# The gate evacuation's walk order: key by key instead of token by token

## The chip, the cores and the metric

The kernel runs on one core of a Trainium2 chip. The metric is the device time of one execution in microseconds (us), the median of several runs. Engines are called as in the profile: PE is the matrix engine (TensorE), PEld its weight loads, DVE is VectorE, ACT is ScalarE, POOL is GpSimd, SP is SyncE; ACTq and SPq are the queues on which ACT and SP issue their DMA transfers. A line of the kernel is written L1143.

## The reference, cut to what matters

The program is one step of a decoder layer for 512 prompt tokens and 32 sample tokens (D_MODEL = 1024): a modulated RMSNorm, one input projection, a convolution group and an mLSTM group, an output projection, and then a retrieval layer (PEER) over 128 x 128 single-neuron experts. The change sits in the retrieval layer:

```
q = (xb @ w_pq).reshape(PEER_BLOCK, PEER_HEADS, 2, PEER_DHALF)
s = jnp.einsum('thpd,phnd->thpn', q, sub_keys)
s1, i1 = lax.top_k(s[:, :, 0], PEER_TOPK)
s2, i2 = lax.top_k(s[:, :, 1], PEER_TOPK)
...
top, pos = lax.top_k(cand, PEER_TOPK)
eidx = jnp.take_along_axis(cidx, pos, axis=-1)
gate = jax.nn.softmax(top, axis=-1)
a = jnp.einsum('thkd,td->thk', u_tab[eidx], xb)
act = (jax.nn.gelu(a) * gate)
out = jnp.einsum('thk,thkd->td', act, v_tab[eidx])
```

Each token takes 8 x 16 experts out of 16384, and each has a gate weight.

## The kernel before, in words

For 416 of the 544 tokens the kernel does not gather: it computes the product of the tokens with all 16384 experts and multiplies the result by a gate matrix that is zero where an expert was not retrieved. The remaining 128 tokens are done by gathered rows on DVE (the functions `dot` and `row_add`, on the tile `ug`), threaded between other work.

The expert table comes in 256 blocks of 512 KB (`tab`). ACT makes the rounded high part of each (`t_hi`, L1092, tile `tHi`), POOL the low part (`lo_part`, L612, tile `tLo`), and PE does 24 matmuls of 416 columns per block (`product`, L866). Blocks 0 to 127 (the first half) are the u table: ACT applies gelu to the result (L1133, tile `ga`) and stores it to a scratch tensor in HBM (L1136, `gelu_scratch`). Blocks 128 to 255 are the v table: gelu and gates come back from HBM, are multiplied, and are PE's operands.

The gate matrix is built during blocks 57 to 116 of the first half. There are 52 steps of 8 tokens (`STEP_TOK`), and `gate_steps(n)` spreads them over the blocks, one behind most products and none behind some. In each step DVE makes one-hot tiles (`one_hots`, L1552 to L1556); PE does one matmul of 128 x 128 for each of the 8 tokens (`gate_product`, L876, shown in the trace as 16 instructions) and writes banks 4 and 5 of PSUM, laid out as 8 tokens by 128 keys, keys innermost; ACT then reads both banks and writes the result into the SBUF tile `stage` (L1143). `stage` has the shape [128 partitions, 2, 128 keys, 32 tokens] in float32: tokens are innermost, and the step's 8 tokens are neighbours of each other there. Four steps fill one half of `stage`, and behind the fourth ACT issues a DMA transfer of 2 MB to `gate_scratch` (L1148). There are 13 of these.

The order of ACT's work in a block n is written out by hand: gelu of block n, the high part of block n+3, the issue of the gelu store (L1136), then the gate step's evacuation (L1143), and behind every fourth one the issue of the gate store (L1148). Both stores are issued on ACT's own queue, so an issue that takes long holds up the evacuation behind it. PE's order is: product of block n, then the gate product of the step. The gate product of step st waits until the evacuation of step st-1 is done (`s_gev`, L873), since there is one pair of banks for it.

Of the kernel before, what the change touches and what calls it, by code (L numbers as in the profile page):

```python
# [9 lines left out]
ACT = mybir.ActivationFunctionType  # L10
AXX = mybir.AxisListType.X

P = 128
# [48 lines left out]
STEP_TOK = TB // 4  # L62
# [31 lines left out]
def gate_steps(n):  # L94

    return [st for st in range(NSTEP) if G_FIRST + st * G_SPAN // NSTEP == n]
# [24 lines left out]
def build(nc, a, o):  # L121
    with ExitStack() as ctx:
# [145 lines left out]
        def peer(name, shape, dt=F32):  # L268
            n = 4
            for q in shape[1:]:  # L270
                n *= q
            t = at(name, shape, zp[0], dt)
            zp[0] += -(-n // 32) * 32
            assert zp[0] <= C_AT + 26400, name
            return t
# [14 lines left out]
        stage = peer("stage", [P, 2, NKEY, TB])  # L290
# [16 lines left out]
        ps = ctx.enter_context(nc.psum_tensor("ps", [P, 8, 512], F32))  # L307
# [21 lines left out]
        def sem(name):  # L329
            return ctx.enter_context(nc.semaphore(name))  # L330
# [91 lines left out]
        s_gev = sem("gate_evacuated")  # L422
# [484 lines left out]
        def _(act):  # L907
            link = linker(act, s_ach)
            f = nc.scalar.activation
# [179 lines left out]
            def t_hi(n):  # L1089

                act.wait_ge(s_tab[n % TABS], 16 * (n // TABS + 1))
                nc.scalar.copy(tHi[:, n % SPL], tab[:, n % TABS]).then_inc(s_thi, 1)  # L1092

            def gelu_copy(c):

                act.wait_ge(s_gin[c % 4], 16 * (c // 4 + 1))
                if c >= 2:
                    act.wait_ge(s_alo, c - 1)
                elif c == 0:
                    act.wait_ge(s_gev, NSTEP)  # L1100
                nc.scalar.copy(ps[:, 4 + c % 2, 0:TD], gin[:, c % 4]).then_inc(s_gcp, 1)

            def act_hi(c):

                act.wait_ge(s_a32, c + 1)
                nc.scalar.copy(actHi[c // GRP % 2][:, c % GRP], ps[:, 4 + c % 2, 0:TD]).then_inc(s_ahi, 1)
# [23 lines left out]
            for n in range(NCH):  # L1130
                act.wait_ge(s_prod, n + 1)
                act.wait_ge(s_gas[n % 2], 16 * (n // 2 + 1))
                f(ga[:, n % 2], ps[:, n % 2, 0:TD], ACT.Gelu_apprx_tanh).then_inc(s_gelu, 1)  # L1133
                t_hi(n + 3)
                act.wait_ge(s_gelu, n + 3)
                act.dma_start(ga_dram[n], ga[:, n % 2]).then_inc(s_gas[n % 2], 16)  # L1136
                if n == N_SHUF - 2:
                    act.wait_ge(s_top, NST)
                    f(best[:, 0], best[:, 0], ACT.Exp).then_inc(s_gexp, 1)
                for st in gate_steps(n):  # L1140
                    b, j = st // 4, st % 4
                    act.wait_ge(s_gmm, st + 1)
                    f(stage[:, b % 2, :, STEP_TOK * j:STEP_TOK * (j + 1)].rearrange("p c t -> p t c"),  # L1143
                      ps[:, 4:6, :].rearrange("p b (t c) -> p (b t) c", c=P), ACT.Identity).then_inc(s_gev, 1)
                    if j == 3:
                        act.wait_ge(s_gev, st + 1)
                        act.wait_ge(s_gst2, 16 * (b + 1))
                        act.dma_start(gt_dram[:, :, b, :].rearrange("q p (c t) -> p q c t", c=4),  # L1148
                                      stage[:, b % 2].rearrange("p (q c) t -> p q c t", c=4)).then_inc(s_gst2, 16)
                if n >= NCH - GRP:  # L1150
                    c = n - NCH + GRP
                    if c == 0:
                        gelu_copy(0)
                    gelu_copy(c + 1)
                    act_hi(c)

            for n in range(NCH, NT):
# [3 lines left out]
                c = n - NCH + GRP  # L1161
# [525 lines left out]
```

## Time and profile before

| | |
|---|---|
| median of 3 runs | 1866.88 us (1865.66 to 1868.56) |
| profiled execution, its own time | 1866.18 us |
| its span in the trace | 1864.5 us |
| PE busy | 1780.4 us, 95% of the span |
| POOL busy | 1083.0 us, 58% |
| DVE busy | 1183.9 us, 63% |
| ACT busy | 728.1 us, 39% |
| mean granted TensorE clock | 0.978 of full speed |

The span is the time from the first to the last instruction that the profiler saw; the profiled execution's own time is 1.7 us longer. The busy time of an engine says how much of the span it worked, not whether the end of the program waits for it. For that the profile has the chain of work that ended last, followed back from the last instruction to what released each step, and a list of waits: which engine waited at which line, and for what.

### The profile page before, as it was taken

The numbers are of one execution on the slowest core, as the hardware profiler recorded it, in microseconds if no ns is written. First come the engines' busy times: TensorE is split into PE (matmuls) and PEld (weight loads), VectorE is DVE, ScalarE is ACT, GpSimd is POOL, SyncE is SP. The second block draws the span as 40 slices with busy tenths as digits, with TensorE's granted clock in tenths as the row PEclk, the third lists the DMA queues.
The fourth block names the chain that finished last, engine by engine and source line by source line (L and its number), as shares of the span: only waits on it lengthen the run. The fifth ranks groups of instructions, "written<-read, shape, count | busy, mean of one in ns | idle before, by whom it ended". The sixth has DMA issues, their size and how long they took to land.

```text
span 1864.5 us, 27254 instructions
## 1 busy us (share of the span) xinstructions
PE 1780.4 (95%) x10594; PEld 1698.5 (91%) x10594; DVE 1183.9 (63%) x2350; ACT 728.1 (39%) x983; POOL 1083.0 (58%) x612
## 2 busy tenths in 40 slices
PE   7899999799999999999999998999999999999995
PEld 3899887688999999999999998989999999999995
DVE  3441343627898799985666665446677777777746
ACT  2454232323333333354554544443444444444431
POOL 1667221132337788854554454477877888887851
PEclk9899999899999999999999999999999999999997
DMA  8545121233215888868687786799999999999951
GB/s 273 172 148 170 62 97 57 75 113 103 91 51 163 273 275 281 275 211 276 233 269 242 250 260 217 228 400 369 363 353 357 377 350 377 353 368 361 364 185 48
DMA packets 191200, 442.39 MB, mean 237 GB/s; under 512 B 20064, under 2 KB 106080, under 8 KB 190816
## 3 DMA queue, kind: packets, MB, share of 16 engines
q1 hardware_dynamic: 82320, 251.88, 39.5%
q0 software_dynamic: 36864, 134.23, 19.4%
q10 hardware_dynamic: 71888, 54.53, 8.8%
q8 instruction: 84, 1.38, 0.3%
q14 instruction: 44, 0.36, 0.1%
HBM read 381.42 MB, written 59.17 MB: 236 GB/s over the span
## 4 chain that ended last, share of the span: by engine, by line
PE 87%; DVE 4%; DMA 3%; ACTq 2%; ACT 2%; issue 1%; POOL 1%; SPq 0%; DVEq 0%; POOLq 0%
PE ps L866 57%; PE ps L652 17%; PE ps L876 5%; ACTq L1136 2%; PE ps L672 2%; PE ps L681 1%; DMA gelu_scratch<-ga 1%; PE ps L841 1%; ACT stage L1143 1%; DMA tab<-in_tab 1%; DMA raw<-in_w 1%; ACT tHi L1092 1%; PE ps L764 0%; DMA ug<-in_urows,eidx 0%; PE ps L798 0%
## 5 line engine op out<-in xcount | busy, mean ns | idle before, releaser
L612 POOL TENSOR_TENSOR tLo<-tab,tHi 128x1024 fp32r<-128x1024 f32 x256 | 635.5, 2482 | 357.9 <-ACT tHi L1092 356.5
L1092 ACT CAST tHi<-tab 128x1024 fp32r<-128x1024 f32 x256 | 267.9, 1047 | 331.9 <-PE ps L866 321.1
L866 PE MATMUL ps<-actHi,tLo 128*128 128x416 f32 x1024 | 361.7, 353 | 5.5 <-issue 5.3
L866 PE MATMUL ps<-hHi,tLo 128*128 128x416 f32 x1024 | 364.5, 356 | 0.0
L866 PE MATMUL ps<-hLo,tHi 128*128 128x416 f32 x1024 | 361.6, 353 | 0.0
L866 PE MATMUL ps<-actHi,tHi 128*128 128x416 f32 x1024 | 359.6, 351 | 0.0
L866 PE MATMUL ps<-hHi,tHi 128*128 128x416 f32 x1024 | 358.8, 350 | 0.0
L866 PE MATMUL ps<-actLo,tHi 128*128 128x416 f32 x1024 | 357.4, 349 | 0.0
L600 POOL TENSOR_TENSOR wLo<-raw,wHi 128x1024 fp32r<-128x1024 f32 x53 | 127.7, 2409 | 316.0 <-ACT wHi L930 316.0
L866 PEld LDWEIGHTS ps<-actHi,tLo 128*128 128x128 f32 x1024 | 192.5, 188 | 7.6 <-issue 5.6
L866 PEld LDWEIGHTS ps<-hHi,tHi 128*128 128x128 f32 x1024 | 193.2, 189 | 2.8
L866 PEld LDWEIGHTS ps<-actLo,tHi 128*128 128x128 f32 x1024 | 192.9, 188 | 2.9
L866 PEld LDWEIGHTS ps<-hHi,tLo 128*128 128x128 f32 x1024 | 193.1, 189 | 1.5
L866 PEld LDWEIGHTS ps<-hLo,tHi 128*128 128x128 f32 x1024 | 192.4, 188 | 1.6
L866 PEld LDWEIGHTS ps<-actHi,tHi 128*128 128x128 f32 x1024 | 193.1, 189 | 0.8
L652 PE MATMUL ps<-hHi,wLo 128*128 128x272 f32 x848 | 180.9, 295 | 11.5 <-DVE hLo L1200 7.9
L1427 DVE SCALAR_TENSOR_TENSOR ug<-ug,ps 128x1024 f32<-128x1024 f32 x128 | 154.9, 1217 | 57.2 <-DMA ug<-in_urows,eidx 56.3
L1133 ACT ACTIVATE ga<-ps 128x416 f32<-128x416 f32 x128 | 66.7, 521 | 310.1 <-PE ps L866 282.0
L1589 DVE SCALAR_TENSOR_TENSOR xT<-ps,mod,xT 128x416 f32<-128x416 f32 x128 | 83.3, 651 | 152.3 <-PE ps L866 152.3
L652 PE MATMUL ps<-hHi,wHi 128*128 128x272 f32 x848 | 176.9, 290 | 0.0
L652 PE MATMUL ps<-hLo,wHi 128*128 128x272 f32 x848 | 176.6, 290 | 0.0
L1437 DVE SCALAR_TENSOR_TENSOR ps<-ug,act_s,ps 128x1024 f32<-128x1024 f32 x127 | 162.8, 1282 | 3.7 <-DVE ps L1437 0.5
(310 smaller groups left out, 2617.8 us busy)
## 6 DMA issues: line engine op xcount, KB each, us to landing
tab<-in_tab SPq DMA_DIRECT2D x256, 512.0 KB, 6.1
raw<-in_w SPq DMA_DIRECT2D x101, 512.0 KB, 3.9
gelu_scratch<-ga ACTq DMA_DIRECT2D x128, 208.0 KB, 4.4
gate_scratch<-stage ACTq DMA_DIRECT2D x13, 2048.0 KB, 14.1
gt<-gate_scratch SPq DMA_DIRECT2D x32, 832.0 KB, 5.8
gin<-gelu_scratch SPq DMA_DIRECT2D x128, 208.0 KB, 7.8
xT<-in_xT SPq DMA_DIRECT2D x1, 2176.0 KB, 10.0
out_y<-yo SPq DMA_DIRECT2D x8, 272.0 KB
```

The lines of the kernel that those rows point to most:

```text
L600: pool.tensor_tensor(wLo[:, i % 2], raw[:, p % RAW], wHi[:, i % 2].bitcast(F32), ALU.subtract).then_inc(s_wlo, 1)
L612: pool.tensor_tensor(tLo[:, n % SPL], tab[:, n % TABS], tHi[:, n % SPL].bitcast(F32), ALU.subtract).then_inc(s_tlo, 1)
L652: last = mm(pair(n)[:, h], w, x[:, k, h * HF:(h + 1) * HF], start=first, stop=end)
L672: last = mm(ps[0:NSEQ, mod_bank(m), 0:2 * P], cT[:, k, :], raw[:, p:p + 2, k, :], start=(k == 0), stop=(k == KT - 1))
L866: last = mm(ps[:, bank, 0:TD], w, x[:, k, 0:TD], start=first, stop=end)
L876: last = mm(out, oh2[:, st % 2, t, :], w1[:, st % 2, t, :], start=True, stop=True)
L1092: nc.scalar.copy(tHi[:, n % SPL], tab[:, n % TABS]).then_inc(s_thi, 1)
L1133: f(ga[:, n % 2], ps[:, n % 2, 0:TD], ACT.Gelu_apprx_tanh).then_inc(s_gelu, 1)
L1136: act.dma_start(ga_dram[n], ga[:, n % 2]).then_inc(s_gas[n % 2], 16)
L1427: stt(ug[:, slot], ug[:, slot], 1.0, h_rows, ALU.mult, ALU.mult, accum_out=a_s[:, q:q + 1]).then_inc(s_item, 1)
L1437: stt(y_rows, ug[:, slot], act_s[:, k:k + 1], y_rows, ALU.mult, ALU.add).then_inc(s_item, 1)
L1589: stt(xT[:, k, 0:TD], ps[:, late_bank(s), 0:TD], mod[:, 5 * KT + k, 0:1], xT[:, k, 0:TD], ALU.mult, ALU.add).then_inc(s_flush, 1)
```

## The change

One instruction in the ACT program changes, 52 times executed. It reads the same 1024 float32 elements per partition from PSUM and writes the same values to the same places in `stage`. Only the order in which it walks over them changes. Before, the outer loop is over the 8 tokens and the inner one over the 128 keys: it reads neighbouring PSUM elements, and each write is 32 elements (128 bytes) behind the one before. After, the outer loop is over the 128 keys and the inner one over the 8 tokens: it writes 8 neighbouring elements (32 bytes) at a time, and each read is 128 elements (512 bytes) behind the one before.

```
                     act.wait_ge(s_gmm, st + 1)
-                    f(stage[:, b % 2, :, STEP_TOK * j:STEP_TOK * (j + 1)].rearrange("p c t -> p t c"),
-                      ps[:, 4:6, :].rearrange("p b (t c) -> p (b t) c", c=P), ACT.Identity).then_inc(s_gev, 1)
+                    f(stage[:, b % 2, :, STEP_TOK * j:STEP_TOK * (j + 1)],
+                      ps[:, 4:6, :].rearrange("p b (t c) -> p c (b t)", c=P), ACT.Identity).then_inc(s_gev, 1)
```

No other instruction, wait, tile or transfer changes.

## Rows read from the trace of the kernel before

**Rows 1.** The page's chain that ended last, shares of the span by line
```profile
PE ps L866 57%; PE ps L652 17%; PE ps L876 5%; ACTq L1136 2%; PE ps L672 2%; PE ps L681 1%; DMA gelu_scratch<-ga 1%; PE ps L841 1%; ACT stage L1143 1%; DMA tab<-in_tab 1%; DMA raw<-in_w 1%; ACT tHi L1092 1%; PE ps L764 0%; DMA ug<-in_urows,eidx 0%; PE ps L798 0%
```

**Rows 2.** Windows, gate stretch: us, busy PE, PEld, DVE, ACT, POOL, clock, DMA, GB/s
```profile
813.50:1204.60 391.10, 371.57 (x2249) 365.47 (x2250) 241.47 (x257) 189.93 (x169) 187.50 (x107) 0.98 0.74 241
```

**Rows 3.** Waits from 812 to 1210 us: total us, times, longest us
```profile
ACT ga L1133 <- PE ps L866: 110.1, 45, 4.4
ACT stage L1143 <- issue: 57.8, 11, 6.9
...
PE ps L876 <- ACT stage L1143: 19.5, 9, 4.1
```

**Rows 4.** Timeline of ACT around the first gate store, and the tenth
```profile
834.61 2.13 ACT L1143 ACTIVATE stage<-ps 128x1024 f32<-128x1024 f32 x1 [0.33 <-PE ps L876]
836.76 0.41 ACTq L1148 DMA_DIRECT2D gate_scratch<-stage  x1
839.16 0.52 ACT L1133 ACTIVATE ga<-ps 128x416 f32<-128x416 f32 x1 [2.43 <-PE ps L866]
...
839.71 4.60 ACTq L1136 DMA_DIRECT2D gelu_scratch<-ga  x1
844.35 1.98 ACT L1143 ACTIVATE stage<-ps 128x1024 f32<-128x1024 f32 x1 [3.74 <-issue]
...
1109.61 0.41 ACTq L1148 DMA_DIRECT2D gate_scratch<-stage  x1
...
1112.56 7.78 ACTq L1136 DMA_DIRECT2D gelu_scratch<-ga  x1
```

**Rows 5.** Timeline of PE: the nine gate products that waited, and the first v-table product
```profile
846.48 2.02 PE L876 MATMUL ps<-w,oh 128*128 128x128 f32 x16 [1.01 <-ACT stage L1143]
...
879.22 3.34 PE L876 MATMUL ps<-w,oh 128*128 128x128 f32 x16 [2.61 <-ACT stage L1143]
...
938.33 2.02 PE L876 MATMUL ps<-w,oh 128*128 128x128 f32 x16 [2.00 <-ACT stage L1143]
...
995.85 3.60 PE L876 MATMUL ps<-w,oh 128*128 128x128 f32 x16 [2.04 <-ACT stage L1143]
...
1029.87 3.65 PE L876 MATMUL ps<-w,oh 128*128 128x128 f32 x16 [2.34 <-ACT stage L1143]
...
1088.18 2.02 PE L876 MATMUL ps<-w,oh 128*128 128x128 f32 x16 [1.22 <-ACT stage L1143]
...
1122.40 3.47 PE L876 MATMUL ps<-w,oh 128*128 128x128 f32 x16 [4.09 <-ACT stage L1143]
...
1151.57 2.68 PE L876 MATMUL ps<-w,oh 128*128 128x128 f32 x16 [2.12 <-ACT stage L1143]
...
1185.37 2.02 PE L876 MATMUL ps<-w,oh 128*128 128x128 f32 x16 [2.08 <-ACT stage L1143]
...
1259.72 0.69 PE L866 MATMUL ps<-actHi,tLo 128*128 128x416 f32 x1 [5.25 <-issue]
```

**Rows 6.** Windows over two of those gate products (columns as in Rows 2)
```profile
879.20:882.60 3.40, 3.38 (x17) 3.40 (x18) 0.00 (x0) 1.15 (x2) 2.17 (x1) 0.57 0.94 354
938.30:940.40 2.10, 2.07 (x18) 2.10 (x19) 0.01 (x1) 1.17 (x3) 0.87 (x1) 1.00 1.08 395
```

**Rows 7.** L1143 alone: ns min/median/max, then first and last start
```profile
L1143 ACT ACTIVATE stage<-ps x52: 1877/2120/2136, 815.6 to 1200.1; 128x1024 f32<-128x1024 f32 x52
```

**Rows 8.** Groups of ACT by shape: busy us, mean ns of one, idle before
```profile
L1092 ACT CAST tHi<-tab 128x1024 fp32r<-128x1024 f32 x256 | 267.9, 1047 | 331.9 <-PE ps L866 321.1 <-DMA tab<-in_tab 10.8
...
L1133 ACT ACTIVATE ga<-ps 128x416 f32<-128x416 f32 x128 | 66.7, 521 | 310.1 <-PE ps L866 282.0 <-DMA gelu_scratch<-ga 18.5 <-issue 9.6
...
L1112 ACT ACTIVATE sc<-ps 128x640 f32<-128x640 f32 x16 | 11.3, 708 | 1.0 <-PE ps L841 1.0
```

**Rows 9.** Timeline of PE: first and last of eleven matmuls in a row
```profile
843.03 0.35 PE L866 MATMUL ps<-hHi,tLo 128*128 128x416 f32 x1
...
844.92 0.35 PE L866 MATMUL ps<-hHi,tHi 128*128 128x416 f32 x1
```

## The prediction

> **What bounds the kernel now.** I read the chain of work that ended last first. Its shares by line [rows 1] are PE's nearly everywhere: the table products (L866) carry 57% of the span. ACT's evacuation L1143 stands in the chain with 1% and the issue of the gelu store (L1136) with 2%, so ACT is not the bound, but it gets onto the path at times. The windows say where: in the stretch of the gate steps, 391.10 us long, PE is busy for 371.57 us at a granted clock of 0.98 [rows 2]. So 19.5 us of PE's time are missing there, and a little is lost to the clock. The list of waits of the same stretch names the cause: PE waited 19.5 us, in 9 places, for ACT's evacuation, which is the whole of the missing time [rows 3]. In the same stretch ACT waited for PE 45 times and sat 57.8 us in 11 places before L1143 on "issue", that is, behind an issue on its own queue [rows 3].
>
> The timeline shows how the two belong together [rows 4]. In an ordinary step the evacuation takes 2.13 us and ACT then idles 2.43 us until PE's next product is done; 2.43 us is the cover of an evacuation in the 43 or so steps that PE does not wait for. Behind every fourth step the gate store is issued (836.76). The next issue on that queue, the gelu store, then takes 4.60 us instead of its usual part of a microsecond: it ends at 844.31, 7.55 us behind the gate store's issue. Only then does the next evacuation start (844.35), and PE's gate product waits for its end. At the tenth store the same distance is 10.73 us (1109.61 to 1120.34). There are 13 stores, and nine of them lead to a wait of PE, from 1.01 to 4.09 us each [rows 5].
>
> **What the change removes, adds and moves.** It adds no instruction, wait or transfer. It changes the duration of 52 evacuations; their values and places stay, so the transfer of `stage` stays too. The question is twofold: how long does the new walk take, and what is a microsecond of it worth.
>
> *The new duration.* Today it is 1.88 us at the least and 2.12 us in the middle [rows 7]. ACT's instructions whose two sides are both walked in neighbouring elements cost 521 ns for 416 elements and 708 ns for 640, both out of PSUM, so 0.83 ns per element; extended to 1024 elements that is 1.03 us, and the SBUF cast of 1024 elements takes 1.05 us [rows 8]. So the old walk costs 0.8 to 1.1 us over the plain one. Its read is plain and its write is the only strided side, so the surplus belongs to the write, and the change takes it away: writes come in runs of 8. What the trace does not show is a strided read of PSUM. Its bounds are 1.04 us (nothing lost) and, as the nearest row with one strided side, 1.88 to 2.12 us (it costs what the strided write costs). A worse end cannot be excluded, since the steps of the read are four times as wide (512 bytes against 128): I put it at twice today's cost per element, 3.3 ns, which gives 3.6 us. I take 1.04 us. The reason is a row of PE: eleven matmuls of 416 columns start 1.89 us apart from first to last, 0.189 us each, so PSUM takes a float32 column in each partition every 0.45 ns [rows 9]. If it does this in accesses of two neighbours, one access takes 0.91 ns, close to ACT's 0.83 ns per element, and an access per element would hold ACT up by little.
>
> A rule of the Trainium skill speaks against this value. "SBUF — State Buffer", section "Door 1: The DMA port swizzle", says of its cachelines that SBUF has lines of 16 bytes and wants two hits on a line for full bandwidth, and that PSUM's lines are only 8 bytes, where a pattern of non-neighbours slows matmuls down. For the old write the trace agrees (2.12 us against 1.05 us). Carried over to ACT's reads, the new read hits each PSUM line once and would be as slow; the time by that rule would be that of the second case below.
>
> *What it is worth in an ordinary step.* Nothing: 2.43 us of idle time lie behind it, and PE runs on. If the evacuation were 2.4 us longer, that cover would be gone.
>
> *What it is worth behind a gate store.* Twice. The fourth step's evacuation ends 2.12 - 1.04 = 1.08 us earlier, so the gate store is issued 1.08 us earlier, and with it the end of the long issue, if the distance between them belongs to the store's own work. Then the waited-for evacuation is itself 1.88 - 1.04 = 0.84 us shorter. Together 1.92 us at each of the nine places, but no more than PE waits there: seven waits are 2.00 us or longer and give 7 x 1.92 = 13.4 us, the two short ones give all they have, 1.01 + 1.22 us. Sum: 15.7 us of the 19.5.
>
> *The clock.* A gate product behind a wait takes 2.02 us in four of the nine places, and 3.34, 3.60, 3.65, 3.47 and 2.68 us in the others [rows 5]. The granted clock in the window over the 3.34 us one is 0.57, near the lower level of 1.2 GHz, against 1.00 (2.4 GHz) over one that took 2.02 us [rows 6]. The slow ones stand behind waits of 2.61, 2.04, 2.34, 4.09 and 2.12 us, the fast ones behind 1.01, 2.00, 1.22 and 2.08 us: so a wait of some 2.0 us or more costs a further 0.7 to 1.6 us. With 1.92 us off, only the wait of 4.09 us stays above (2.2 us). The excess over 2.02 us is 1.32 + 1.58 + 1.63 + 1.45 + 0.66 = 6.6 us; the 1.45 stays, 5.2 us come back.
>
> *Behind the stretch.* The last gate store is 1.08 us earlier against PE too. PE's next long wait is 5.25 us, before the first product of the v table [rows 5], behind a tangle of transfers; some of the 1.08 us may come off it. I take nothing. What is late next is nothing new: DVE's one-hots wait for PE and move with it, and POOL's low parts get their input from the cast before the evacuation, not behind it.
>
> Sum: 15.7 + 5.2 = 20.9 us. Against the profiled execution (1866.18 us) this gives 1845.3; the median of the runs is 0.7 us higher, so 1846.0.
>
> **The rivals.**
>
> *The store's end doesn't move.* If the long issue ends when other traffic lets it (its distance to the gate store varies from 7.55 to 10.73 us [rows 4], which speaks for some of this), only the 0.84 us of the waited-for evacuation count: 9 x 0.84 = 7.6 us. The waits fall below 1.8 us except for the longest, so the clock gives its 5.2 us as well: 12.8 us, 1854.1 us.
>
> *The stride only changes sides.* The read costs what the write did, 1.88 to 2.12 us. At the ends of that: if the evacuation is 1.88 us everywhere, the gate store comes 0.24 us earlier and nine times that is 2.2 us; nothing else moves. So 1864.7 to 1867, no change that can be told. This is the case in which the change does not do what it says. For it: both walks have one side with one element per access. Against it: PE's rate of writing.
>
> *The strided read is dearer than the strided write.* At 3.6 us per evacuation the ordinary step still fits (1.5 us more against a cover of 2.43 us), but behind a store both effects turn round: 1.48 us by the later store and 1.72 us by the longer evacuation, 3.2 us at each of nine places, 28.8 us; and the four gate products that run at full clock today would come behind waits of 4 us and lose some 1.5 us each, 6 us. Together 34.8 us, 1901.7 us, and more where the four other stores join in. It decides early: at 9 x 2x = 3.7 us, so from x = 0.21 us of longer evacuation on, the kernel is slower than can be mistaken.
>
> **How the numbers follow.** I give 0.45 to the full gain, 0.13 to the smaller one (12.8 us), 0.27 to the stride that changes sides, 0.15 to the dearer read. A measurement of this kernel can tell about 0.2% (3.7 us) from no change. Faster: the first two and a little of the third, whose read may come out between the ends (at 1.4 us it already gains some 10 us): 0.60. Within 0.2%: 0.25. Slower: 0.15. The likeliest case's own range is 1841 to 1855 (from all of the 19.5 us and the clock, to the smaller gain). The range that is to hold 8 times in 10 has to take in the third case and leaves out the fourth: 1840 to 1869.
>
> **What the profile of the changed kernel would show.** The duration of L1143 decides first: some 1.04 us (likeliest), about 1.9 to 2.1 us (stride changed sides), 2.4 us or more (slower). Second, the distance from a gate store's issue to the end of the next gelu store's issue: still 7.5 to 10.7 us if it belongs to the store, longer by about a microsecond if it doesn't. Third, PE's wait for L1143: from 19.5 us to about 4, with at most one or two gate products longer than 2.1 us, and a clock nearer 1.0 in the stretch. The stretch itself should be some 370 us long. The prediction is wrong if the strided read costs more than 1.5 us, if the DMA issues rearrange themselves against the faster PE, or if the wait before the v table grows by what the gate stretch gives up, since that stretch of transfers has its own pace.

## The result and the profile after

The changed kernel takes 1836.30 us (median of 4 runs, 1835.45 to 1837.33) against 1866.27 us for the kernel before in the same comparison (1864.32 to 1868.56): a ratio of 0.984, 95% interval 0.9825 to 0.9856, 30.0 us less. The forecast was 1846.0 us, 20.9 us less, and the range 1840 to 1869: right in direction, too small by almost a third, and the time lies below the range. A second comparison on another occasion gave 1838.88 us for the changed kernel, a ratio of 0.9851 (the runs are reported with the experiments).

The evacuation itself, L1143 alone in the changed kernel (ns min/median/max, first and last start):

```profile
L1143 ACT ACTIVATE stage<-ps x52: 1024/1027/1038, 813.1 to 1169.9; 128x1024 f32<-128x1024 f32 x52
```

1.03 us in place of 2.12 [rows 7]: a read of PSUM with a step of 512 bytes costs nothing that can be seen over the 1.03 us that the plain reads extend to [rows 8]. This was the most doubtful term of the forecast, and it came out at its lower bound.

The page's chain of work that ended last, by line (against [rows 1]):

```profile
PE ps L866 62%; PE ps L652 18%; PE ps L876 5%; PE ps L672 2%; PE ps L681 1%; PE ps L841 1%; DMA raw<-in_w 1%; PE ps L764 0%; ACTq L1136 0%; PE ps L798 0%; DVE rs L1206 0%; PE ps L786 0%; PE ps L774 0%; DVE hf L1195 0%; PE ps L741 0%
```

L1143 is gone from it, and the gelu store's issue L1136 went from 2% to 0%. The waits from 812 to 1180 us, total us, times, longest us (against [rows 3]):

```profile
ACT stage L1143 <- issue: 27.6, 10, 4.7
...
PE ps L876 <- ACT stage L1143: 1.3, 2, 0.7
```

PE's waits for the evacuation went from 19.5 us to 1.3. The two that are left, in the timeline of PE (against the nine of [rows 5]):

```profile
873.59 2.02 PE L876 MATMUL ps<-w,oh 128*128 128x128 f32 x16 [0.69 <-ACT stage L1143]
...
1099.95 2.02 PE L876 MATMUL ps<-w,oh 128*128 128x128 f32 x16 [0.60 <-ACT stage L1143]
```

The windows from the first gate product to the start of the last one, and from there to the first v-table product (columns as in [rows 2]), after and then before:

```profile
811.00:1169.90 358.90, 357.56 (x2225) 353.89 (x2226) 241.62 (x257) 136.37 (x168) 185.52 (x107) 1.00 0.79 262
1169.90:1227.40 57.50, 54.44 (x290) 53.61 (x288) 22.96 (x40) 26.20 (x43) 43.31 (x28) 1.00 1.00 371
```

```profile
813.50:1200.05 386.55, 367.02 (x2225) 360.98 (x2226) 241.47 (x257) 187.83 (x168) 185.32 (x107) 0.98 0.74 243
1200.05:1259.70 59.65, 54.42 (x288) 53.57 (x288) 22.98 (x40) 27.21 (x42) 44.95 (x29) 0.99 0.98 366
```

The gate stretch gives 386.55 - 358.90 = 27.7 us. PE has the same 2225 rows in both windows; 18.2 us of the 27.7 are its waits (19.5 - 1.3), the other 9.5 us are its own busy time, 367.02 - 357.56, with the granted clock up from 0.98 to 1.00. The stretch behind it gives 59.65 - 57.50 = 2.2 us. Together 29.8 us before rounding, about the difference of the medians. (The two profiled executions differ by 30.7 us. What is over comes from two places that the change doesn't touch: the first gate product comes 2.5 us earlier in the one after, and from the first v-table product on it takes 1.5 us longer.)

One thing the forecast had taken as fixed was not. The timeline of ACT around the fourth gate store:

```profile
918.20 1.03 ACT L1143 ACTIVATE stage<-ps 128x1024 f32<-128x1024 f32 x1 [0.33 <-PE ps L876]
919.26 0.38 ACTq L1148 DMA_DIRECT2D gate_scratch<-stage  x1
922.76 0.52 ACT L1133 ACTIVATE ga<-ps 128x416 f32<-128x416 f32 x1 [3.53 <-PE ps L866]
...
923.30 3.02 ACTq L1136 DMA_DIRECT2D gelu_scratch<-ga  x1
926.37 1.03 ACT L1143 ACTIVATE stage<-ps 128x1024 f32<-128x1024 f32 x1 [2.16 <-issue]
```

From the gate store's issue to the end of the next issue on the queue it is 7.06 us here (923.30 + 3.02 - 919.26). The same store had 8.63 us before (930.58 + 5.68 - 927.63):

```profile
927.63 0.41 ACTq L1148 DMA_DIRECT2D gate_scratch<-stage  x1
...
930.58 5.68 ACTq L1136 DMA_DIRECT2D gelu_scratch<-ga  x1
```

I call this the distance. Over the 13 stores its mean went from 8.99 to 7.41 us, worked out in the same way from the timelines; it is shorter at 12 of them. The next load of 512 KB for the table is what had moved against the store. Around the tenth store of the kernel before (1109.61 [rows 4]), the low part whose end releases the table load, and the load's issue on SP's queue:

```profile
1107.20 2.42 POOL L612 TENSOR_TENSOR tLo<-tab,tHi 128x1024 fp32r<-128x1024 f32 x1 [1.02 <-ACT tHi L1092]
```

```profile
1109.64 0.33 SPq L517 DMA_DIRECT2D tab<-in_tab  x1
```

It was issued 0.03 us behind the gate store. In the changed kernel, around the store at 919.26 (two loads merged into one row, which begins with the first):

```profile
920.38 6.67 SPq L517 DMA_DIRECT2D tab<-in_tab  x2
```

Now the store is 1.12 us ahead of the load. The same holds at every store: the load is issued 0.03 to 0.05 us behind each of the 13 before, and 1.12 us or 1.13 us behind each of the 13 after. I call this the store's head start. Whether the head start or something else shortens the distance is what the experiments had to tell.

### The profile page after: what moved, and what is told of

It is laid out like the page before. It is cut to its first block, busy times and chain, and to the rows that moved or that the text cites. A ratio compares the mean times of both kernels' runs of the same rounds, so it can differ in the third digit from the quotient of the medians.

```text
span 1833.7 us, 27254 instructions
## 1 busy us (share of the span) xinstructions
PE 1770.7 (97%) x10594; PEld 1691.8 (92%) x10594; DVE 1183.2 (65%) x2350; ACT 675.5 (37%) x983; POOL 1085.3 (59%) x612
## 4 chain that ended last, share of the span: by engine, by line
PE 93%; DVE 4%; issue 1%; ACT 1%; DMA 1%; ACTq 0%; POOL 0%; SPq 0%; DVEq 0%; POOLq 0%
PE ps L866 62%; PE ps L652 18%; PE ps L876 5%; PE ps L672 2%; PE ps L681 1%; PE ps L841 1%; DMA raw<-in_w 1%; PE ps L764 0%; ACTq L1136 0%; PE ps L798 0%; DVE rs L1206 0%; PE ps L786 0%; PE ps L774 0%; DVE hf L1195 0%; PE ps L741 0%
## 5 line engine op out<-in xcount | busy, mean ns | idle before, releaser
L866 PE MATMUL ps<-actLo,tHi 128*128 128x416 f32 x1024 | 362.0, 354 | 0.0
L652 PE MATMUL ps<-hHi,wLo 128*128 128x272 f32 x848 | 180.9, 295 | 11.5 <-DVE hLo L1200 7.9
```

The lines of the kernel that those rows point to most:

```text
L652: last = mm(pair(n)[:, h], w, x[:, k, h * HF:(h + 1) * HF], start=first, stop=end)
L866: last = mm(ps[:, bank, 0:TD], w, x[:, k, 0:TD], start=first, stop=end)
```

## The experiments

Ratios are against the kernel before, run beside the variant on the same chip. Theories. **A**: only the time that ACT is held counts, through its queue: the store's moment against the table load sets the distance, and distance and evacuation together set PE's wait. **B**: the strided writes disturb others whatever time they take. **C**: the distance has nothing to do with the table load. The distances quoted below are means over the 13 stores of one profiled execution, from the timelines. Executions with the same head start of 1.12 us differ by 0.3 us in this mean (7.41 to 7.71), so smaller differences are read store by store.

**A pad in front of every evacuation.** Edit to the changed kernel:

```
+                    act.wait_ge(s_pad, pads[0])
+                    f(pad[:], ps[:, 4:6, :].rearrange("p b (t c) -> p c (b t)", c=P), ACT.Identity).then_inc(s_pad, 1)
+                    pads[0] += 1
                     f(stage[:, b % 2, :, STEP_TOK * j:STEP_TOK * (j + 1)], ...).then_inc(s_gev, 1)
```

> The changed kernel, with an extra ACT copy of the same shape in front of every one of the 52 evacuations (the same strided read of PSUM, written to a spare tile in neighbouring elements). So ACT is held some 2.05 us per step, as before the change, but writes nothing in strides. Theory A (only ACT's time counts): PE's waits for the evacuation come back, 19.5 us plus 9 x 0.17 us, some 21 us, the clock loss of some 8 us too, and the time is 1866 us, within 4 us. Rival B (strided writes disturb the other engines or the transfers, whatever time they take): the time stays below 1845 us.

Measured: 1855.79 us, ratio 0.995 (0.9931 to 0.9969), so 10 us below the kernel before: a third of the gain was still there. Neither expectation was met. PE's waits were 14.4 us in 9 places, not 21, and only one gate product took longer than 2.1 us (2.83). The distance was 8.41 us. The reason may be that the pad and the evacuation overlap and end 1.94 us from the start of the pad, so that the store still has a head start of 0.21 us over the table load; or it may be theory B. The next run tells these apart.

**The pad made longer, by 0.2 us as it turned out.**

```
-                    f(pad[:], ps[:, 4:6, :].rearrange(...), ACT.Identity).then_inc(s_pad, 1)
+                    f(pad[:], ident[:, 0:16].unsqueeze(1).broadcast_to([P, 77, 16]), ACT.Identity).then_inc(s_pad, 1)
```

> As the pad in front of all 52 evacuations, but the extra ACT copy is 1232 elements long (from a constant in SBUF to the spare tile, neighbouring writes), some 0.17 us longer, so that the gate store is issued at the same moment against the table load as before the change (0.0 us, not 0.17 us ahead of it), and the evacuation ends 2.1 to 2.2 us behind its start. Theory A (ACT's time and nothing else): the distance goes from 8.4 to 9.0 us, PE's waits from 14.4 to 20 us, the time to 1866 us within 4. Rival B (the strided writes themselves cost something as well): distance and time stay near those of the shorter pad, 1856 to 1859 us (0.17 us more at nine places makes 1.5 to 3 us).

Measured: 1869.27 us, ratio 1.0025 (1.0007 to 1.0043). The whole gain is gone, with no strided write in the kernel: theory B is out as a cause of any size. The head start is 0.00 us, the distance 8.84 us (8.99 in the kernel before), and it is longer than with the shorter pad at all 13 stores. PE's waits are 22.2 us, 2.7 us more than the 19.5 of the kernel before; that fits theory A, since pad and evacuation together take 2.15 us behind a long issue, where the old evacuation took 1.88 us with PE standing still. The slow gate products are back. The wait row of the shorter pad, the one of the longer, and three of the longer's gate products:

```profile
PE ps L879 <- ACT stage L1150: 14.4, 9, 2.3
```

```profile
PE ps L879 <- ACT stage L1150: 22.2, 9, 4.4
```

```profile
878.71 3.64 PE L879 MATMUL ps<-w,oh 128*128 128x128 f32 x16 [2.83 <-ACT stage L1150]
...
1028.79 3.65 PE L879 MATMUL ps<-w,oh 128*128 128x128 f32 x16 [2.65 <-ACT stage L1150]
...
1121.86 3.76 PE L879 MATMUL ps<-w,oh 128*128 128x128 f32 x16 [4.40 <-ACT stage L1150]
```

0.2 us more of ACT per step (2.15 us against 1.94) cost 13.5 us: 7.8 us of waits, and some 5.3 us because four gate products (3.14 to 3.76 us) ran slow in place of one. I had allowed 10.

**The pad only in front of the fourth evacuation** (the store is late, the waited-for evacuation short; `if j == 3:` around the pad).

> The extra ACT copy only in front of the fourth step's evacuation, the one that the gate store waits for. The store is issued 1.03 us later, at the moment of the table load, as before the change; the evacuation behind the long issue stays short (1.03 us). Theory A (the store's distance to the end of the next issue depends on whether the table load of 512 KB is issued with it or 1.1 us behind it): the distance goes from a mean of 7.4 us back to some 9.0 us, PE's waits are 19.5 - 9 x 0.84 = some 12 us, three or four of them with a clock drop, and the time is 1850 us, within 4. Rival C (the distance has nothing to do with the table load and stays at 7.4 us): waits of some 3.5 us, 1839 us.

Measured: 1846.41 us (1844.89 to 1851.94), ratio 0.9896 (0.9871 to 0.992). The distance is back at 8.67 us, with a head start of 0.21 us (not 0.0 as expected, for the reason given above). PE's waits are 9.5 us in 7 places, with one slow gate product (3.75 us); I had expected some 12 us and 1850. The time is inside the expected range, and rival C (3.5 us, 1839) is out. The trace is of the slowest of the four runs, 1851.94 us, so the median run probably waited less.

**The pad only in front of the first evacuation of four** (`if j == 0:`; the store is early, the waited-for evacuation long).

> The extra ACT copy only in front of the first evacuation of each four, the one that comes behind the long issue. The store stays early, and the distance stays at 7.4 us in the mean by Theory A and Rival C alike; the waited-for evacuation takes 2.05 us in place of 1.03. Only distances above some 7.5 us then reach PE: about 3.5 us of waits, 1839 us, within 3. If the two halves were worth the same, as the prediction put it, this would cost as much as the pad in front of the fourth.

Measured: 1837.31 us (1835.78 to 1838.34), ratio 0.9848 (0.9824 to 0.9871), within a microsecond or so of the changed kernel. Distance 7.58 us, one wait of 2.4 us. Starting from the changed kernel, then, a late store costs 10 us and a long evacuation behind the stall 1, which cannot be told from nothing. With an early store the long issues mostly end before PE gets there.

The three padded kernels and the changed one together show that the halves do not add up, and that neither has a worth of its own:

| | evacuation behind the stall 1.03 us | 1.94 us |
|---|---|---|
| head start 1.12 us | 1836.30 (changed kernel) | 1837.31 (pad first) |
| head start 0.21 us | 1846.41 (pad fourth) | 1855.79 (pad in front of all) |

With a late store the long evacuation costs another 9.4 us. (The pad in front of all also lengthens the second and third evacuation of each four, which PE does not wait for.)

**The kernel before, with the table loads held back.** The evacuation stays strided; only the load is issued later.

```
                     sp.wait_ge(s_tlo, n - TABS + 1)
+                if G_FIRST + 6 <= n < NCH - 4:
+                    sp.wait_ge(s_prod, n - 5)
```

> The kernel before the change (strided writes, 2.1 us), with the table loads of the gate stretch held back until PE has finished one product more, so that they are issued some 2.4 us behind the gate store and not with it. Theory A (head start over the table load): the distance shrinks from 9.0 us to 7.5 us or less, PE's waits from 19.5 to some 7 us, and with the clock the time is some 1847 us, within 6. Rival C (the table load doesn't matter): the distance stays at 9.0 us and the time at 1866 us, or longer if tables come late.

Measured: 1843.67 us (1842.94 to 1845.46), ratio 0.9886 (0.9862 to 0.9909): 22 us of the 30 with the old evacuation. ACT and SP around the fourth store:

```profile
918.55 2.12 ACT L1145 ACTIVATE stage<-ps 128x1024 f32<-128x1024 f32 x1 [0.33 <-PE ps L878]
920.70 0.38 ACTq L1150 DMA_DIRECT2D gate_scratch<-stage  x1
...
923.65 3.98 ACTq L1138 DMA_DIRECT2D gelu_scratch<-ga  x1
```

```profile
923.14 6.67 SPq L519 DMA_DIRECT2D tab<-in_tab  x2
```

```profile
PE ps L878 <- ACT stage L1145: 7.2, 6, 3.0
```

The load comes 2.44 us behind the store, the distance of this store is 6.93 us in place of 8.63, the mean 7.15 in place of 8.99, and PE waits 7.2 us. All 13 distances are shorter than before. PE still waits longer than in the changed kernel (1.3 us), since the store is as late and the evacuation as long as before. The shorter distance is the work of the head start alone: nothing but the table loads was moved. How a load on SP's queue lengthens an issue on ACT's is not shown by any run.

**The kernel before, with the gate stores on SP's queue.**

```
+            def gates_out(b):
+                sp.wait_ge(s_gev, 4 * (b + 1))
+                sp.wait_ge(s_gst2, 16 * (b + 1))
+                sp.dma_start(gt_dram[:, :, b, :]..., stage[:, b % 2]...).then_inc(s_gst2, 16)
...
                 table(n)
+                for st in gate_steps(n - 7):
+                    if st % 4 == 3:
+                        gates_out(st // 4)
...
-                        act.dma_start(gt_dram[:, :, b, :]..., stage[:, b % 2]...).then_inc(s_gst2, 16)
```

> The kernel before the change with the 13 gate stores issued by SP, on the queue of the table loads, so that no issue on ACT's queue is long. Theory A: the evacuations still take 2.1 us, and that costs nothing: PE's waits for them fall from 19.5 us to below 1, the gate stretch loses some 27 us, the time is 1838 us within 5, unless tables come late behind the stores on SP's queue (then 5 to 15 us more, with PE or ACT waiting for tables). Rival D (a 2.1 us evacuation is itself too long somewhere): waits stay above 5 us.

Measured: 1837.12 us (1835.01 to 1837.45), ratio 0.9843 (0.981 to 0.9877). ACT also gets a wait, not shown above, before it writes a half of `stage` whose store may still be under way. SP and ACT around the first gate store, where ACT's queue had been blocked in the kernel before [rows 4], and the evacuation's group (busy us, mean ns of one, idle before):

```profile
833.68 0.38 SPq L529 DMA_DIRECT2D gate_scratch<-stage  x1
```

```profile
836.14 0.33 ACTq L1150 DMA_DIRECT2D gelu_scratch<-ga  x1
837.37 2.11 ACT L1159 ACTIVATE stage<-ps 128x1024 f32<-128x1024 f32 x1 [0.33 <-PE ps L890]
```

```profile
L1159 ACT ACTIVATE stage<-ps 128x1024 f32<-128x1024 f32 x52 | 110.1, 2117 | 18.9 <-PE ps L890 18.9
```

All 52 evacuations still take 2.12 us, PE never waits for one, and the time is that of the changed kernel. The gelu store's issue behind each gate store takes 0.33 us; the long issue has moved to SP's queue, where the table load behind each store now takes 1.8 to 3.7 us to issue in place of 0.33, and in the gate stretch neither ACT nor PE waited for a table. So a long evacuation costs time only where a blocked queue has made it late.

**The changed kernel with the same move, and with the table loads held back.**

> The same move of the gate stores to SP's queue in the changed kernel. Only 1.3 us of waits are left there, so at most some 2 us are to be had: 1834 to 1838 us. With the same stores, it should be within 2 us of the kernel before with this move.

Measured: 1836.44 us (1835.63 to 1837.91), ratio 0.9838 (0.9804 to 0.9872), as expected: once the queue is free the new walk adds nothing.

> The changed kernel with the table loads of the gate stretch held back by one product. They are then issued 3.5 us behind the gate store. The long issues shrink by another 0.5 to 1 us in the mean, the last two waits of PE (1.3 us together, with two pipeline refills of 0.24 us) go: 1834 to 1836 us.

Measured: 1833.87 us (1833.81 to 1835.64), ratio 0.9829 (0.9794 to 0.9863), distance 6.87 us, no wait of PE for an evacuation left. Whether that is below the changed kernel was asked again, five runs each on one chip.

> The changed kernel once more, beside the next one on the same chip: 1836 us, within 2 us.

> The changed kernel with the table loads held back by one product, again. It was 2.4 us below the changed kernel's median on another occasion. By Theory A it takes away PE's last 1.3 us of waits and two pipeline refills of 0.24 us: 1 to 3 us below the changed kernel on the same chip. If it is within 0.5 us, the gain of that step is not real.

Measured: the changed kernel 1838.88 us (1833.93 to 1839.62), ratio 0.9851 (0.9834 to 0.9868), outside the 2 us that I had given it; its trace has a distance of 7.71 us and waits of 3.1 us in two places, against 7.41 and 1.3 in the first. With the loads held back 1835.65 us (1834.99 to 1837.90), ratio 0.9846 (0.983 to 0.9862). The medians are 3 us apart in the expected direction, but the runs overlap, and so do the intervals. A version that beats the changed kernel is not established.

**What the write costs.** Two forms of the new walk that write shorter runs, one run each. Runs of 4 go bank by bank:

```
+                    f(stage[...].rearrange("p c (b t) -> p b c t", t=4),
+                      ps[:, 4:6, :].rearrange("p b (t c) -> p b c t", c=P), ACT.Identity)
```

> The evacuation walks each bank key by key with its 4 tokens innermost: writes in runs of 4 neighbours (16 bytes), reads 512 bytes apart. If only single writes are dear, it takes 1.03 us as with runs of 8.

Runs of 2 go over four pairs of tokens:

```
+                    f(stage[...].rearrange("p c (h t) -> p h c t", t=2),
+                      ps[:, 4:6, :].rearrange("p b (h t c) -> p (b h) c t", t=2, c=P), ACT.Identity)
```

> Writes in runs of 2 neighbours (8 bytes). If the cost is one access of SBUF for each run and two of ACT's cycles hide it, it takes 1.03 us again and the time is that of the changed kernel, 1836 us; if every run costs a cycle more, 1.45 us, with the time between 1836 and 1850 us.

Measured: the groups, first with runs of 4, then of 2:

```profile
L1143 ACT ACTIVATE stage<-ps 128x1024 f32<-128x1024 f32 x52 | 53.4, 1026 | 46.1 <-issue 30.2 <-PE ps L876 15.9
```

```profile
L1143 ACT ACTIVATE stage<-ps 128x1024 f32<-128x1024 f32 x52 | 59.6, 1146 | 47.4 <-issue 31.8 <-PE ps L876 15.5
```

1.03 us with 4 neighbours (as expected), 1.15 us with 2, against 2.12 us for single elements. Times of 1838.60 and 1835.62 us, both about that of the changed kernel; a single run each tells no more. Neither of the two guesses for 2 was met (1.03 or 1.45): it is nearer the first.

## Why the prediction came out too small, point by point

The step that failed is the second half's premise, that the end of the long issue moves with the store because the distance between them belongs to the store's own work; in its place the runs showed a distance that shrinks as the store gets ahead of the table load (8.99 to 7.41 us in the mean, and 7.15 us when nothing but the loads was moved). The larger part of the miss is of size: 4.3 us more than forecast of what comes back with PE's waits (clock and overlap), and 2.2 us behind the stretch.

- **PE bounds the kernel, and 19.5 us of its waits are ACT's**: right, and closed by the windows.
- **The new duration, 1.04 us**: right (1.03). The case for it was weak (PE's rate of writing to PSUM), and nothing here shows that this is the reason, so the choice of 1.04 us over 2.12 was in part luck. The rule on cachelines that was weighed against it (the Trainium skill, "SBUF — State Buffer", section "Door 1: The DMA port swizzle") fits SBUF's side: one hit per line is dear, two or more nearly free (2.12, 1.15, 1.03 us). For PSUM it speaks of matmuls, and ACT's reads with one element per line do not follow it.
- **An ordinary step is worth nothing**: right; the 2.12 us evacuation with a free queue costs nothing at all.
- **Twice 0.84 to 1.08 us behind a gate store, 15.7 us**: the step that failed in kind. It rested on "if the distance between them belongs to the store's own work", and the rival to it let the end stay where it was, with a distance longer by about a microsecond as its sign. Neither is so: the end moved by more than the store did. The distance depends on how far the table load is behind the store, and shrank by 1.6 us in the mean (1.3 in the second trace of the changed kernel). The waits gave 18.2 us. Nor do the two halves add up: undoing the early store alone costs 8 to 10 us, undoing the short evacuation alone about 1, undoing both 19.5 (1855.79 against 1836.30).
- **The clock, 5.2 us**: right in kind, mis-sized; it measured 9.5 us. The 4.09 us wait was to stay above 2 us and keep its 1.45 us; it fell with the rest. I took 2.02 us as the price of an undisturbed gate product, but in the chain one without a wait takes 1.78 us, since in the trace it starts before the matmul ahead of it has ended; any wait of PE costs these 0.24 us as well, at seven places 1.7 us. And the products right behind a slow gate product were slow too, 1.2 us. 5.2 + 1.45 + 1.7 + 1.2 = 9.5. The rule that I had read off, slow behind a wait of some 2.0 us or more, does not hold: with the longer pad gate products behind waits of 2.30, 2.37 and 2.44 us took 2.02 us, and with the shorter one a product behind 1.84 us took 2.83 (rows below).
- **Behind the stretch, nothing taken**: 2.2 us came (a wait of 5.25 us before, 3.06 after). I had seen this wait and that the last store would be earlier against PE, but the traces speak against that link: with the table loads held back in the kernel before, the store is as late as ever and the wait is 3.07 us, and the second trace of the changed kernel has 4.22 us. What sets this wait stays open, and 2.2 us is the figure of one pair of executions.

One gate product of the longer pad, one of the shorter, and the first v-table product of the kernel before with the loads held back and of the changed kernel's second trace:

```profile
996.03 2.02 PE L879 MATMUL ps<-w,oh 128*128 128x128 f32 x16 [2.37 <-ACT stage L1150]
```

```profile
1171.72 2.83 PE L879 MATMUL ps<-w,oh 128*128 128x128 f32 x16 [1.84 <-ACT stage L1150]
```

```profile
1235.75 0.68 PE L868 MATMUL ps<-actHi,tLo 128*128 128x416 f32 x1 [3.07 <-issue]
```

```profile
1230.78 0.68 PE L866 MATMUL ps<-actHi,tLo 128*128 128x416 f32 x1 [4.22 <-issue]
```

In sum: 20.9 + 2.5 (waits) + 4.3 (clock and lost overlap) + 2.2 (behind) = 29.9 us, of rounded terms. The lower end of the range, 1840, held no such case because it took the sum of the visible waits as a ceiling and priced their consequences short.

## What to carry to other kernels

Ask what a shorter instruction releases and what that is issued against: here the evacuation's duration cost nothing where ACT's queue was free, but it decided how far a 2 MB store was issued ahead of a 512 KB load, and 0.2 us of it was worth 13 us. Savings that meet at one wait do not add: a shorter evacuation behind the stall was worth 9 us with a late store and about 1 with an early one. When a compute engine issues large transfers from its own queue, the next issue can hold that engine for microseconds; moving the transfer to another queue took away the same 29 us as the faster instruction. And price a wait of PE with all that hangs on it (the wait, the lost overlap, the slow clock behind it): here 18.2 us of waits came with 9.5 us of the rest.

## What the runs showed of the hardware

- ACT reads PSUM with a step of 512 bytes between elements as fast as neighbouring elements: 1.03 us for 1024 per partition, and 1.03 us is what the plain reads of 416 and 640 elements extend to [rows 8]. Single float32 writes to SBUF 128 bytes apart cost twice as much, 2.12 us in the middle [rows 7] and 1.88 us in the seven places where PE stands still all the while; runs of 2 cost 1.15 us, runs of 4 or 8 1.03 us.
- The distance from the issue of a 2 MB store to the end of the next issue on its queue depends on another queue: 8.84 and 8.99 us in the mean with a 512 KB load issued at the same moment, 8.41 and 8.67 us with the load 0.21 us behind, 7.41 to 7.71 us at 1.12 us, 7.15 us at 2.44 us, 6.87 and 6.96 us at 3.54 us. Single stores range from 5.3 to 11.5 us.
- PE's gate product took 2.02 us behind waits of 0.4 to 2.44 us, and 2.7 to 3.8 us behind waits of 1.84 to 4.4 us; the granted clock over one of the slow ones was 0.57, near the lower of the two levels [rows 6]. Between 1.84 and 2.44 us both happen, so the length of the wait alone does not tell.
